# Expert gate and up weights by whole-matrix transfers in a one-core hybrid encoder step

## What is computed

```python
def expert_block(args):
    rows, e = args
    xb = hp[rows]                      # up to 128 token rows, 1024 wide
    a = xb @ p['moe_w_gate'][e]        # 1024 x 512
    v = xb @ p['moe_w_up'][e]          # 1024 x 512
    return (jax.nn.silu(a) * v) @ p['moe_w_down'][e]   # 512 x 1024
```

## Time and profile before

| | us |
|---|---|
| three runs | 1188.43, 1191.17, 1192.58 |
| median | 1191.17 |
| profiled execution, span from the first to the last instruction | 1191.2 |
| TensorE busy | 1106.2 |
| VectorE busy | 439.0 |
| ScalarE busy | 249.8 |

### The profile page before, as it was taken

The page is one execution under the profiler, slowest core; times in us unless marked ns, Lnnn a source line. Parts: engine busy times, 40 slices in busy tenths (PEclk is TensorE's granted clock), DMA queues, the critical chain, the costliest instruction groups (busy, mean ns, idle before and its releaser), DMA issues.

```text
span 1191.2 us, 17482 instructions
## 1 busy us (share of the span) xinstructions
PE 1106.2 (93%) x7024; PEld 538.6 (45%) x7024; DVE 439.0 (37%) x1048; ACT 249.8 (21%) x488; POOL 113.7 (10%) x202
## 2 busy tenths in 40 slices
PE   6999999999998999999989999989999998998645
PEld 3666666767754564555553333323333332332211
DVE  3589998380047762323352210101011100110017
ACT  3300012102553872322120000000000000000007
POOL 0000000000055000000320010000100100010016
PEclk9999999899999999999989999999999999999978
DMA  7121124004001104000978999999999999999868
GB/s 292 36 98 38 35 73 73 1 1 123 14 21 65 83 1 168 36 35 36 371 257 276 411 415 357 413 413 414 377 410 411 405 415 412 411 411 414 346 234 326
DMA packets 73491, 271.84 MB, mean 228 GB/s; under 512 B 10625, under 2 KB 15425, under 8 KB 65345
## 3 DMA queue, kind: packets, MB, share of 16 engines
q1 hardware_dynamic: 67200, 252.61, 55.4%
q0 software_dynamic: 6048, 17.83, 3.8%
q10 hardware_dynamic: 160, 0.26, 0.1%
HBM read 251.18 MB, written 23.55 MB: 231 GB/s over the span
## 4 chain that ended last, share of the span: by engine, by line
PE 59%; DVE 17%; DMA 8%; SPq 8%; ACT 4%; issue 3%; POOL 0%; POOLq 0%; DVEq 0%; ACTq 0%
PE psA L1154 17%; PE psB L1183 9%; DVE psC L1708 7%; SPq L571 6%; PE psA L1004 4%; PE psB L1004 4%; DMA arena<-in_w_down 4%; PE psA L680 3%; PE psB L680 3%; PE psC L805 3%; PE psA L824 2%; DMA arena<-in_w_up 1%; DMA arena<-hn_rows,ints 1%; PE psC L1139 1%; DVE arena L1708 1%
## 5 line engine op out<-in xcount | busy, mean ns | idle before, releaser
L1154 PE MATMUL psA<-arena 128*32 128x512 f32 x2688 | 299.4, 601 | 20.0 <-DMA arena<-in_w_up 18.2
L1154 PEld LDWEIGHTS psA<-arena 128*32 128x32 f32 x2688 | 86.8, 111 | 215.2 <-issue 211.9
L1183 PE MATMUL psB<-arena 128*32 128x512 f32 x1344 | 150.9, 599 | 11.5 <-DMA arena<-in_w_down 11.5
L680 PE MATMUL psA<-arena 128*128 128x360 f32 (+1 forms) x384 | 122.6, 478 | 11.4 <-DVE arena L1585 11.4
L2157 DVE TENSOR_TENSOR arena<-psA,arena 128x512 f32<-128x512 f32 x21 | 14.5, 692 | 317.1 <-ACT arena L1524 317.1
L680 PE MATMUL psB<-arena 128*128 128x360 f32 (+1 forms) x384 | 121.9, 477 | 0.0
L680 PEld LDWEIGHTS psA<-arena 128*128 128x128 f32 x384 | 73.7, 194 | 55.6 <-issue 14.1
L680 PEld LDWEIGHTS psB<-arena 128*128 128x128 f32 x384 | 74.3, 194 | 44.4 <-issue 2.4
L1183 PEld LDWEIGHTS psB<-arena 128*32 128x32 f32 x1344 | 42.8, 110 | 104.1 <-issue 102.0
L1708 DVE SCALAR_TENSOR_TENSOR psC<-arena,params,psC 128x1024 f32<-128x1024 f32 x70 | 89.8, 1283 | 0.0
L1524 ACT ACTIVATE arena<-psA 128x512 f32<-128x512 f32 x21 | 12.5, 597 | 307.1 <-PE psA L1154 307.1
(11 more groups left out here) (437 smaller groups left out, 1184.9 us busy)
## 6 DMA issues: line engine op xcount, KB each, us to landing
arena<-in_w_gate SPq DMA_DIRECT2D x128, 512.0 KB, 13.7
arena<-in_w_up SPq DMA_DIRECT2D x128, 512.0 KB, 16.7
arena<-in_w_down SPq DMA_DIRECT2D x64, 1024.0 KB, 15.0
arena<-in_w_cm SPq DMA_DIRECT2D x16, 512.0 KB, 3.6
arena<-expert_rows SPq DMA_DIRECT2D x16, 512.0 KB, 10.5
arena<-in_xT SPq DMA_DIRECT2D x8, 544.0 KB, 10.0
arena<-in_w_out SPq DMA_DIRECT2D x1, 4096.0 KB, 12.6
arena<-in_x_rows SPq DMA_DIRECT2D x8, 512.0 KB, 7.7
```

Of the source, the lines that this page charges most:

```text
L680: mm = te.matmul(AB[j % 2][:, 512 * b:512 * b + hi - lo], wring[:, j % 4, k * P:(k + 1) * P], xn[:, k, lo:hi], start=(k == 0), stop=(k == ...
L1154: mm = te.matmul(psA[tile, at:at + FF], xgT[:, k, tile], w[o % RG][:, k, :], start=(k == 0), stop=(k == KT - 1))
L1183: mm = te.matmul(psB[tile, n * 512:(n + 1) * 512], hT[:, k * P + c * TW:k * P + c * TW + TW], w, start=(k == 0), stop=(k == 3))
```

## The change

Gate and up weights come by one transfer per matrix. `GC` becomes 2: part 0 is all of gate, part 1 all of up. A transfer has 2 MB, 16 KB per partition in one piece, and an expert has two of them. TensorE runs all eight k with gate, then all eight with up. ScalarE's SiLU waits for part 0 alone, VectorE's product also for part 1. A place's gate half is free after part 0 of the last block that used it, its up half after part 1. The number of matmuls, bytes and row transfers stays.

```diff
-RG, RD, GC, DC = 3, 2, 4, 2
+RG, RD, GC, DC = 3, 2, 2, 2
-GK, DK = KT // GC, 4 // DC
+GU_PART = [(m, slice(h * 2 * KT // GC, (h + 1) * 2 * KT // GC)) for m in range(2) for h in range(GC // 2)]
+DK = 4 // DC
@@ gate_up_in (SyncE)
-                r, ks = n % RG, slice(c * GK, c * GK + GK)
-                for w, src in ((wg[r], a["w_gate"]), (wu[r], a["w_up"])):
-                    sp.dma_start(w[:, ks, :], src[ds(e, 1), :, :].rearrange("o (p k) n -> (o p) k n", k=KT)[:, ks, :]
-                                 ).then_inc(s_wgu[r][c], 16)
+                r, (m, ks) = n % RG, GU_PART[c]
+                w, src = ((wg[r], a["w_gate"]), (wu[r], a["w_up"]))[m]
+                sp.dma_start(w[:, ks, :], src[ds(e, 1), :, :].rearrange("o (p k) n -> (o p) k n", k=KT)[:, ks, :]
+                             ).then_inc(s_wgu[r][c], 16)
@@ gate_up (TensorE)
-                        te.wait_ge(s_wgu[o % RG][part], 32 * (o // RG + 1))
-                    for k in range(part * GK, part * GK + GK):
-                        for w, at in ((wg, 0), (wu, FF)):
-                            for c, o in enumerate(QUADS[q]):
-                                tile = slice(c * TW, c * TW + TW)
-                                mm = te.matmul(psA[tile, at:at + FF], xgT[:, k, tile], w[o % RG][:, k, :],
-                                               start=(k == 0), stop=(k == KT - 1))
+                        te.wait_ge(s_wgu[o % RG][part], 16 * (o // RG + 1))
+                    m, ks = GU_PART[part]
+                    for k in range(ks.start, ks.stop):
+                        for c, o in enumerate(QUADS[q]):
+                            tile = slice(c * TW, c * TW + TW)
+                            mm = te.matmul(psA[tile, m * FF:(m + 1) * FF], xgT[:, k, tile], (wg, wu)[m][o % RG][:, k, :],
+                                           start=(k == 0), stop=(k == KT - 1))
@@ activated (ScalarE)
-                ac.wait_ge(m_gu, GC * (q + 1))
+                ac.wait_ge(m_gu, GC * q + GC // 2)
@@ multiplied (VectorE)
                 ve.wait_ge(m_sil, q + 1)
+                ve.wait_ge(m_gu, GC * (q + 1))
```

## The result

The changed kernel takes 1256.61 us (median of 4 runs, 1251.59 to 1261.28) against 1189.8 us for the kernel before (median of 4, 1182.61 to 1192.58): a ratio of 1.0568, 95% interval 1.0524 to 1.0613. It is slower, as forecast, but by 67 us where 23 were forecast, and outside the range. In this and in all later executions the time is some 2 us above the span, so that span and median of the kernel before agreed by chance. The spans differ by less than the medians because the profiled execution of the changed kernel was the fastest of its four.

A forecast was written before the change was run, and what follows sets the result against it. Expert-stage blocks were taken to alternate between TensorE-paced and weight-paced, with DMA engines near their limit. 1191.2 + 32 (late rows, clock falls) - 9 (weight waits gone) = 1214 us, range 1184 to 1240 for 8 in 10.

The forecast's parts named there:

- part 2: Rows beside weights: queues alternate by packet, so gathers land after 16.1 us, due after 11.8; +32 us with clock falls.
- the place of the wait: TensorE's transposes (line 1139) would wait for gathered rows, some 30 to 45 us in total.
- the end of the waits for gate and up weights: TensorE's waits for gate and up weights, 18.2 us before, would come under 10 us.
- the DMA share under 1: Sign of a right forecast: a DMA share clearly under 1 in the expert stage.
- 17 turns: A gather waits 17 times for one weight piece; with 16 KB pieces each turn is 0.30 us longer, 5.1 together.
- Part 1: Gate and up weights in 16 KB pieces need 14.5 us less DMA time; bounds nothing and 20.9.
- Part 3: From block 20 on, weights come early because rows pace the blocks, so TensorE's waits for them go: -9 us.
- How often?: In the expert stage, two of three blocks have late rows and take 27.1 us, the third 22.8.
- rival (d): Slower still: every one of 16 blocks has late rows and takes 27.1 + 0.8 us: 1241 us; chance 0.08.
- the clock term: TensorE's clock falls after every second new wait for rows: 0.8 us a late block, bounds 0 and 1.6.
- Part 4: Waits and release by whole matrices: covered by ready weights once rows pace the blocks; uncovered, 3.5 us in a block.
- Rival (a): Faster: larger pieces pay and rows keep pace; 14.5 us back, less 3.5 and 3.5: 1184 us; chance 0.18.

The follow-up runs named there:

- run 2: Changed kernel with each gate and up matrix in two transfers of 8 KB pieces: 1192.17 us, 1.0003 of the kernel before.
- run 1: Changed kernel with each gate and up matrix in four transfers of 4 KB pieces: 1202.3 us, 1.0099 of the kernel before.
- run 3: Changed kernel, 16 KB pieces, with GpSimd issuing the gather of block q + 2 ahead of the scatter of block q - 1: 1185.54 us, 0.9939.
- run 4: Kernel before the change, with GpSimd issuing the gather of block q + 2 ahead of the scatter of block q - 1: 1188.4 us, 0.9967.
- run 6: Changed kernel with the gather ahead of the scatter and 4 KB pieces, four transfers to a matrix: 1195.81 us, 1.0045 of the kernel before.
- Run 9: Changed kernel with SyncE, from block 4 on, holding gate and up back until that block's gather has landed: 1227.49 us, 1.0341.
- Run 8: Changed kernel with four constant matmuls filling TensorE's wait for gathered rows, from block 5 (counted from 0) on: 1231.05 us, 1.0323.

## Why the prediction went wrong, point by point

**Right**: the mechanism of part 2 (turns by the packet, at 0.61 us for a 16 KB piece, where 80.8% of 12 us of 16 engines for 247 pieces are 0.63; landing after 16.1 us forecast, a median of 15.3 and at most 17.1 measured), the place of the wait, the end of the waits for gate and up weights, and the DMA share under 1. The number of 17 turns, from two gathers, was rather high: from run 2 to the changed kernel the median landing rises by 3.9 us, 13 turns of 0.30. Runs 1 to 4 leave the mechanism as the cause: smaller pieces or an earlier gather take all of the loss away but the 1% of whole-matrix waits. Part 1 was near: 14.5 us of DMA time, 10 measured between runs 6 and 3. Part 3 was right in its sum: from the start of block 20's gate and up to the last down matmul it was 45 us (1098.7 to 1143.7), it is 35.0 now, -10 us for -9. Of the 13.6 us of waits 7.4 went, not 8.9; 1.5 more went with the slow matmuls after the wait of 3.27 us. Its two last waits stayed, as the part had it:

```profile
1166.88 13.94 PE L1155 MATMUL psA<-arena 128*32 128x512 f32 x128
...
1192.17 3.64 PE L1184 MATMUL psB<-arena 128*32 128x512 f32 x32 [3.80 <-DMA arena<-in_w_down]
1198.23 3.64 PE L1184 MATMUL psB<-arena 128*32 128x512 f32 x32 [2.42 <-DMA arena<-in_w_down]
```

**Wrong, the step "How often?"** of part 2. I took two of three blocks as late, by the share of the bytes. The runs show all 16 from block 4 on: TensorE's 63.0 us are 3.9 a block, not 4.3 in two of three, 2.9, which is 16 us over the stage; 30 to 45 us of such waits were forecast. A share of bytes over the whole stage says nothing about one moment of a block, and the trace of before had what was needed: SyncE's order puts gate and up right behind the wait for a down place, and the scatter hangs on the same down matmuls. The same slip is in what I held against rival (d), that the queue cannot stay full. It does not stay full; it is full for most of the 12 us in which the rows move, in every block. That down pieces spare the rows was right (block 3); but the order in the queue decides it block by block, and only three of the 16 had down pieces for as much as half. Run 9 takes most of that meeting away, and the waits with it.

**Wrong, the size of the clock term.** I took a fall at every second late block, 0.8 us. Down matmuls and transposes took 29 us more than before (169.6 and 34.3 against 151 and 24), 1.8 us a block where 0.5 were in the sum (0.8 in two of three), 20 us over the stage. Run 8 got 25.6 of the runs' 67 us back by filling the waits. This term missed by more than the first.

With these two the sum closes: 22.8 + 3.9 + 1.8 = 28.5 us a block, and measured are (1166.88 - 707.47) / 16 = 28.7, where 26.2 were forecast and 24.2 stood before. 16 x 4.5 = 72, less 10 at the end, and less 4 because block 4 began at 707.47 and not 711.47 (2.4 of it before the stage began): 58 us between the spans.

```profile
707.47 13.94 PE L1155 MATMUL psA<-arena 128*32 128x512 f32 x128
```

The prediction's own upper bounds, every block late and 1.6 us of clock in each, give 22.8 + 4.3 + 1.6 = 28.7 and about 1254 us; its range stopped at 1240, so it left out a case that its bounds allowed.

**Part 4** said that waits by whole matrices are covered once rows pace the blocks; with rows in time the kernel is 1% slower (run 1), as much as its 3.5 us in three or four blocks; which blocks pay is not shown. **Rival (a)** would have been right with the gather first (1185.54 for 1184), in part by luck: it had 14.5 us back for the pieces and 7 lost, and the runs give 10 back (6 to 3) and 7 lost (4 to 6). The Trainium skill's rule of at least 1 MiB per DMA, named in part 1, holds here only so: larger transfers, with larger pieces, are worth 10 us once no other queue is delayed by them, and in this kernel as it stood they are a loss.

## What to carry to other kernels

Where two DMA queues share the engines as here, the piece size of the bulk queue sets the latency of the other: about the rows per engine in the other queue x the time of one bulk piece. Before making pieces larger, look up which small transfer is issued at the same moment, how many turns it needs, and how much slack it has; here 0.8 us of slack (11.8 less 11.0) stood against 5 us. Here, too, the order of two issues on the small queue gave back all that the larger pieces had taken.

## What the runs showed that was not expected

One expert's two matrices (16 pieces per engine) are enough to delay a burst of 17 turns by 3.5 us beyond its slack (block 9, the window from 852 us), in a queue that then runs empty: stretches of the changed kernel have a DMA share of 0.84 and the rows are still late. And short waits are dear for the clock:

```profile
640.00:700.00 60.00, 60.00 (x547) 20.29 (x543) 8.28 (x19) 4.13 (x7) 4.05 (x4) 1.00 1.01 420
700.00:800.00 100.00, 87.36 (x740) 29.54 (x736) 11.13 (x19) 6.47 (x11) 8.11 (x8) 0.93 0.91 366
1000.00:1100.00 100.00, 82.19 (x674) 28.00 (x666) 9.77 (x16) 5.30 (x9) 6.07 (x6) 0.90 0.84 341
```

In these stretches (columns as in the earlier trace rows) the granted clock goes from 1.00 to 0.93 and 0.90 with one wait of 1.5 to 5.3 us in each block, and TensorE loses about 1.8 us a block to the lower of its two levels.
